# 24 instead of 32 tokens of the expert stage computed from gathered rows, the other 232 by dense products

## The chip, the cores and the metric

The kernel runs on one core of a Trainium2 chip. The metric is the device time of one execution in microseconds, median of the runs. The inputs are fixed by the reference: 256 tokens of width 1024, float32.

## The reference, cut to what matters

One encoder layer: an input projection, two attentions, gates, an output projection, and then the stage that this change is in, a retrieval of single-neuron experts. Each token picks 16 of 16,384 experts for each of 8 heads (128 picks), with a softmax weight for each pick.

```python
s = jnp.einsum('thpd,hpkd->thpk', q, sub_keys)
v_half, i_half = lax.top_k(s, K)
cand = v_half[:, :, 0, :, None] + v_half[:, :, 1, None, :]
top_s, pos = lax.top_k(cand.reshape(TB, PH, K * K), K)
idx = jnp.take_along_axis(cidx.reshape(TB, PH, K * K), pos, axis=-1)
g = jax.nn.softmax(top_s, axis=-1)
u = expert_u[idx]
a = jax.nn.gelu(jnp.einsum('td,thkd->thk', xb, u), approximate=False)
return jnp.einsum('thk,thkd->td', g * a, expert_v[idx])
```

## The kernel before, in words

**Two ways to the same sum.** Most tokens go the dense way: the activation of every one of the 16,384 experts is computed for them, and what was not picked is multiplied by a gate of 0. NU = 256 - APART = 224 tokens do. The last APART = 32 tokens go apart: their picked rows of `peer_u` and `peer_v` are gathered from HBM by indirect DMAs, 128 rows of 4 KB at a time, and multiplied and added on the VectorE (DVE).

**Dense, first stage (U).** 128 tiles of 128 experts. A tile of 512 KB is loaded to one of four `raw` buffers (SP, `load`, L505), the ScalarE (ACT) rounds it to the high part `whi` (L694), the VectorE or the GpSimd (POOL) subtracts that from it to get the low part `wlo` (L974, L1364 and L1366, L634). TensorE (PE) makes, for each of 8 chunks of the width, three products: high by high, high by low, low by high. In tiles 0 to 41, 126 and 127 these are three matmuls of NU columns (L1524, `split_product`). In tiles 42 to 125 ("wide" tiles) the two products with the same stationary operand are one matmul of 2 x NU columns (L1532), followed by one of NU (L1533): a pair. The two halves of a wide tile are added outside: ACT copies one (L850, `take_half`), DVE adds the other (L1358, `add_halves`), ACT applies the GELU (L839), and SP stores the tile to `a_scratch` (L537).

**The gate matrix G.** For tokens 0 to 127 it is scattered to HBM by 128 indirect DMAs of POOL (L667, L669). For tokens 128 to NU - 1 it is made on PE during the wide tiles: one-hot vectors (L1341, L1346 on DVE, L858 on ACT), two matmuls of 256 columns per two tokens (L1787), a copy by ACT (L893) and an add by DVE (L1353, `add_low`). That is G_STEPS = (128 - APART) / 4 = 24 steps of four tokens, three for every eight tiles, from tile 41 to tile 103. In a tile with neither the one-hots of a step nor an `add_low`, DVE splits its subtraction into two halves with `add_halves` between them (`low_halves`, L1360).

**Dense, second stage (V).** 128 tiles of `peer_v`, through the same four buffers. For each, DVE multiplies activations by gates (L1402, `weights`), ACT rounds (L901), DVE subtracts (L1407, `low`) and makes the low part of the `peer_v` tile (L1411, `v_low`). PE makes for each of 8 chunks the pair of 2 x NU and NU columns (L1836, L1837, `v_products`). In the last three tiles, chunk 7 is three matmuls of NU columns instead (L1839). The load of tile i + 4 into a buffer waits until the low part of tile i is made (`load_v`, L582), and the loads of its activations and its G tile wait for `weights` (`load_a`, L587).

**Apart.** The 32 x 128 picks are laid out on 128 partitions as SHARES = 4 groups of 32 tokens with PICKS = 32 columns. So 32 gathers of `peer_u` rows (L644) with 32 dot products (L1377), and 32 gathers of `peer_v` rows (L650) with 32 scaled adds (L1391 and L1394). Six of the `peer_u` gathers are issued during U. The other 26 and the 32 of `peer_v`, 58 in all, come in V, in the order that the string `V_OPS` gives ("d" a dot, "r" a row), one for every 1.9 tiles. The GELU of the dots is applied in three parts (ENDS, GELU_GROUPS). After tile 120, eight products with a column selector of APART columns (L1870) bring the sum into the accumulators. SP loads the picks (L550, 4 DMAs) and the tokens' own vectors (L557, 4 DMAs) during U.

**Order of the work.** Every engine's program is written out by hand, and the engines meet at semaphores. PE waits in V for `lo_ready` and `glo_ready` of the tile at its start (`v_wait`, L1842). SP issues in program order; in the middle and towards the end of V it also loads `h1` (L613 to L616) for the last residual sum.

```python
for half in range(1 if k is None else 2):
    part = range(C) if k is None else range(half * C // 2, (half + 1) * C // 2)
    if wide_now:
        last = halves_product(dst, [(whi[s][:, c, :], wlo[s][:, c, :], xpair[:, :, c, 0:NU]) for c in part], 0 in part, C - 1 in part)
...
pe.matmul(wide[c], whi[s][:, c, :], gpair[s], start=opening, stop=False)
return pe.matmul(acc[c][:, 0:NU], wlo[s][:, c, :], ghi[s], start=False, stop=closing)
```

Of the kernel before, what the change touches and what calls it, by code (L numbers as in the profile page):

```python
# [34 lines left out]
P = 128  # L35
# [9 lines left out]
PH, NK, TOPK = 8, 128, 16  # L45
# [15 lines left out]
T_U = T_QUERY + HP  # L61
# [26 lines left out]

GTOK = 4
GSUB = 2  # L90
APART = 32
G_STEPS = (P - APART) // GTOK
G_FIRST = 41
G_LAST = G_FIRST + (G_STEPS - 1) // 3 * 8 + (G_STEPS - 1) % 3 * 3
# [11 lines left out]


NU = T - APART
SHARES = 4
PARTS = SHARES * APART  # L110
PICKS = 32
DOTS_U = 6
DOT_TILES_U = (76, 84, 92, 100, 110, 117)
GATHERS_U = {3: (0, 1), 4: (2, 3), 5: (4,), 6: (5,)}
ENDS = (0, 6, 18, 32)
WIDE_FIRST, WIDE_END = 42, 126
PICKS_AT, XROWS_AT = 45, 53
OFFSETS_AT = 52
# [1 line left out]
V_SLOT = 512  # L120
NG = NU - P
G_BLOCK = P + NK // RAW * NG
V_OPS = "ddrddrddrddrddrddr" + "dddd" + "dr" * 10 + "r" * 16
OP_FIRST, GATHER_LEAD = 10, 9
GELU_GROUPS = (2, 12, 22)
A_AHEAD_AT = 96


def op_tile(n):

    return OP_FIRST + n * 19 // 10


DOT_AT = {op_tile(n): DOTS_U + V_OPS[:n].count("d") for n in range(len(V_OPS)) if V_OPS[n] == "d"}
ROW_AT = {op_tile(n): V_OPS[:n].count("r") for n in range(len(V_OPS)) if V_OPS[n] == "r"}
SHARES_AT = tuple(min(t for t in ROW_AT if ROW_AT[t] == m) for m in ENDS[:-1])
H_GROUP = 15
# [9 lines left out]
def wide_tile(i):  # L147

    return WIDE_FIRST <= i < WIDE_END


def g_step_at(i):

    at = i - G_FIRST
    if at < 0 or at % 8 not in (0, 3, 6):
        return None
    k = at // 8 * 3 + at % 8 // 3
    return k if k < G_STEPS else None
# [50 lines left out]
def build(nc, stream, urows, vrows, const, keys, bias, lamv, gfin, h1_dram, x_dram, a_dram, g_dram, out):  # L209
    with ExitStack() as top:  # L210
# [3 lines left out]
        def sem(name):  # L214
            return top.enter_context(nc.semaphore(name))

        def sbs(stack, name, shape, dt=F32):
            return stack.enter_context(nc.sbuf_tensor(name, shape, dt))
# [60 lines left out]
                route = sbs(router, "route", [P, TB, 3, PH, TOPK])  # L279
                gsum = sbs(router, "gsum", [P, 2, TB, PH])  # L280
        G = sbs(top, "G", [P, RAW, G_BLOCK])
        held = sbs(top, "held", [P, 128, NK])
        sbs(top, "v_pad", [P, 32])
        vpair = sbs(top, "vpair", [P, RING, V_SLOT], F32R)
        small = sbs(top, "small", [P, T - P - 122, NK])
# [3 lines left out]
        def piece(at, n):  # L289
            return held[:, at:at + n, :].rearrange("p a b -> p (a b)")  # L290
# [3 lines left out]
        def G_at(s, turn, n):  # L294

            if isinstance(turn, int):
                return G[:, s, (turn - 1) * NG:(turn - 1) * NG + n]
            return G[:, s, bass.ds((turn - 1) * NG, n)]
# [4 lines left out]
        xall = piece(76, 8)  # L303
# [3 lines left out]
        ghi = [vpair[:, s, V_SLOT // 2:V_SLOT // 2 + NU] for s in range(RING)]  # L307
        uoff = small[0:P, 2, 0:PICKS].bitcast(U32)
        dots = small[0:P, 2, PICKS:2 * PICKS]
        shares = small[0:P, 2, 2 * PICKS:3 * PICKS]  # L310
        picks = small[0:P, 5, 0:3 * PICKS].rearrange("p (a k) -> p a k", a=3)
        chosen = small[0:P, 3, 0:APART]
        ident2 = small[:, 4, :]
# [21 lines left out]
        result = hT[:].rearrange("p (b x) t -> p b (x t)", b=TB)  # L335
        xtok = qpad[0:APART, 4:8, :].rearrange("p a t -> p (a t)")
        hots = [hot1[:, u] for u in range(HOTS - 1)] + [hot_more[:]]
# [115 lines left out]
        x_landed_apart = sem("x_landed_apart")  # L453
# [35 lines left out]
        def _(sp):  # L489
# [15 lines left out]
            def load(t, s, row):  # L505

                sp.wait_ge(lo_ready, t - RAW + 1)
                sp.dma_start(raw[s][:], row).then_inc(raw_landed[s], 16)
# [25 lines left out]
            def store(i, s2):  # L534

                sp.wait_ge(evac_act, i + (act_takings(T_U) + 1))
                sp.dma_start(a_dram[i] if isinstance(i, int) else a_dram[bass.ds(i, 1)], ast[s2][:]).then_inc(a_stored[s2], 16)  # L537

            def stored(i):

                sp.wait_ge(a_stored[i % AST], 16 * (i // AST + 1))


            def load_picks(g):

                if g == 0:
                    sp.wait_ge(routed, 1)
                n = min(PICKS, PH * TOPK - g * PICKS)
                mine = route[P - APART:P, 1].rearrange("p a h k -> p a (h k)")[:, :, g * PICKS:g * PICKS + n]
                sp.dma_start(picks[g * APART:(g + 1) * APART, :, 0:n], mine).then_inc(picks_landed, 16)  # L550

            def load_xrows(g):

                if g == 0:
                    sp.wait_ge(xtok_stored, 16)
                    sp.wait_ge(gbanks_free, 2)
                sp.dma_start(xall[g * APART:(g + 1) * APART], x_dram).then_inc(x_landed_apart, 16)  # L557

            for t in range(T_U, T_V):
                load(t, t % RAW, stream[t])  # L560
                if t >= T_U + STORE_LAG:
                    store(t - T_U - STORE_LAG, (t - T_U - STORE_LAG) % AST)
                if t == T_U + 1:
                    sp.wait_ge(xtok_ready, 1)
                    sp.dma_start(x_dram, xtok).then_inc(xtok_stored, 16)
                if 0 <= t - T_U - A_AHEAD_AT < 4:
                    q = t - T_U - A_AHEAD_AT
                    stored(q)
                    sp.dma_start(aring[q], a_dram[q]).then_inc(a_landed[q], 16)
                if 0 <= t - T_U - PICKS_AT < SHARES:  # L570
                    load_picks(t - T_U - PICKS_AT)
                if 0 <= t - T_U - XROWS_AT < SHARES:
                    load_xrows(t - T_U - XROWS_AT)
            for s in range(RAW):
                load(T_V + s, s, vrows[s:s + 1])
                i = NE_TILES + s - STORE_LAG
# [14 lines left out]
            for s in range(RAW):  # L591
                load_v(RAW + s, s)
                i = NE_TILES + RAW + s - STORE_LAG
# [33 lines left out]
        def _(pool):  # L627
# [44 lines left out]
            for q in range(4):  # L672
                pool.dma_start(G_at(q, 1, P), g_tiles[q]).then_inc(g_first[q], 16)
            for n in range(len(V_OPS)):
                at = op_tile(n)
# [12 lines left out]
        def _(act):  # L688
# [227 lines left out]
            def gelu_dots(part):  # L916

                act.wait_ge(dots_done, ENDS[part + 1])
                at = slice(ENDS[part], ENDS[part + 1])
                act.activation(dots[:, at], dots[:, at], ACT.Gelu).then_inc(dots_gelu, 1)  # L920

            first = 1
            for part, end in enumerate(GELU_GROUPS):
                groups(first, end)
# [35 lines left out]
        def _(dve):  # L960
# [285 lines left out]
            split = SHORT_X * TOPK  # L1246
# [121 lines left out]
            def offsets_apart():  # L1368

                dve.wait_ge(picks_landed, 16 * SHARES)  # L1370
                dve.scalar_tensor_tensor(uoff, picks[:, 0, :], float(NK), picks[:, 1, :], ALU.mult, ALU.add).then_inc(uoff_ready, 1)

            def dot(j):

                dve.wait_ge(x_landed_apart, 16 * SHARES)
                dve.wait_ge(urow_landed[j % U_BUFS], 16 * (j // U_BUFS + 1))
                dve.scalar_tensor_tensor(urow[j % U_BUFS], urow[j % U_BUFS], 1.0, xall, ALU.mult, ALU.mult, accum_out=dots[:, j:j + 1]).then_inc(dots_done, 1)  # L1377

            def gates_apart(part):

                dve.wait_ge(dots_gelu, part + 1)
                at = slice(ENDS[part], ENDS[part + 1])
                dve.tensor_tensor(shares[:, at], picks[:, 2, at], dots[:, at], ALU.mult).then_inc(shares_ready, 1)

            def add_row(m):

                row = urow[U_BUFS + m % V_BUFS]
                dve.wait_ge(shares_ready, sum(m >= e for e in ENDS[:-1]))
                dve.wait_ge(urow_landed[U_BUFS + m % V_BUFS], 16 * (m // V_BUFS + 1))
# [37 lines left out]
            more_low(T_U + G_FIRST + LO_LEAD - at_lo[0])  # L1427
            for i in range(G_FIRST, NE_TILES):
                before, ahead = g_step_at(i - 1), g_step_at(i + 2)
                split = wide_tile(i - 1) and ahead is None and before is None  # L1430
                if wide_tile(i - 1) and not split:
                    add_halves(i - 1)
                if ahead is not None:
                    one_hots(2 * ahead)
                if before is not None:
                    add_low(before)
                if i == NE_TILES - 1:
                    low(0, 0)
                    low(1, 1)
                if split:  # L1440
                    low_halves(T_U + i + LO_LEAD, i - 1)
                else:
                    low_w(T_U + i + LO_LEAD)
                if ahead is not None:
                    one_hots(2 * ahead + 1)
                j = dot_at(i)
                if i == OFFSETS_AT:
                    offsets_apart()
                if j is not None:
                    dot(j)  # L1450
                if i == G_LAST + 1:
                    dve.wait_ge(gbanks_free, 2 + G_STEPS)
                    dve.wait_ge(g_done, 2 * G_STEPS)
                if i == NE_TILES - 2:
                    weights(0, 0, 1)
                    weights(1, 1, 1)
# [536 lines left out]
```

## Time and profile before

| what | value |
|---|---|
| median of 3 runs | 928.15 us (925.18 to 928.76) |
| the profiled execution | 928.84 us |
| its span, first to last instruction | 927.0 us |
| PE busy | 914.0 us |
| PE weight loads busy | 877.7 us |
| DVE busy | 806.1 us |
| ACT busy | 572.5 us |
| POOL busy | 402.7 us |
| moved by DMA | 261.33 MB |

The profiled execution takes 1.8 us outside its span. Matmuls are pipelined and a recorded matmul is longer than the time until the next one starts, so that a busy PE is not yet a PE at its peak: what a matmul costs in a stream is the distance between starts. The weight loads (PEld) are recorded apart and overlap the matmuls.

### The profile page before, as it was taken

What the parts mean: (1) busy time and instruction counts of PE and PEld (TensorE: products, weight loads), DVE (VectorE), ACT (ScalarE), POOL (GpSimd) and SP (SyncE); (2) the same over time, 40 slices, a digit from 0 to 9 for tenths busy, and PEclk for the clock granted to TensorE, in tenths of its full rate; (3) what the DMA queues carried; (4) which work ended last, traced back from release to release, by engine and by line L of the source; (5) the groups of instructions that cost most, each with busy time, mean ns of one, the idle gap of its engine ahead of it and who ended that gap; (6) DMA issues with size and microseconds to landing.
All of it is one profiled execution on the core that took longest, in us unless ns stands there. A gap on an engine that the chain in (4) does not pass through costs nothing.

```text
span 927.0 us, 20169 instructions
## 1 busy us (share of the span) xinstructions
PE 914.0 (99%) x6644; PEld 877.7 (95%) x6644; DVE 806.1 (87%) x1654; ACT 572.5 (62%) x1059; POOL 402.7 (43%) x234
## 2 busy tenths in 40 slices
PE   9999999999999999999999999999999999999997
PEld 8999889999999999999999999999999899999997
DVE  7988877887799997888999876789999899999886
ACT  6555774666645556888788766555555455555555
POOL 0000000047697786888878867222224223243400
PEclk9999999999999999999999999999999999999999
DMA  8877658566477888999999999999999999999991
GB/s 301 264 236 214 206 176 263 188 225 213 158 250 231 242 242 203 265 285 279 237 256 250 264 261 257 310 402 398 394 381 360 400 394 387 397 338 402 394 306 47
DMA packets 137592, 261.33 MB, mean 282 GB/s; under 512 B 31184, under 2 KB 80208, under 8 KB 137264
## 3 DMA queue, kind: packets, MB, share of 16 engines
q1 hardware_dynamic: 110544, 225.72, 72.6%
q0 software_dynamic: 26544, 33.89, 13.8%
q10 hardware_dynamic: 432, 0.80, 0.3%
q8 instruction: 40, 0.66, 0.3%
q14 instruction: 32, 0.26, 0.1%
HBM read 234.94 MB, written 25.36 MB: 281 GB/s over the span
## 4 chain that ended last, share of the span: by engine, by line
PE 74%; DVE 9%; DMA 7%; issue 4%; ACT 4%; SPq 1%; another core or an unknown queue 0%; DVEq 0%; ACTq 0%
PE pOO L1524 29%; PE pMM L1532 5%; PE pOO L1532 5%; PE pTT L1836 4%; DMA raw<-in_vrows 4%; PE pOO L1836 4%; PE pMM L1836 4%; PE pSS L1836 4%; PE pMM L1533 3%; PE pOO L1533 2%; ACT whis L694 2%; PE pMM L1837 2%; PE pOO L1837 2%; PE pTT L1837 2%; PE pSS L1837 2%
## 5 line engine op out<-in xcount | busy, mean ns | idle before, releaser
L694 ACT ACTIVATE whis<-raw 128x1024 fp32r<-128x1024 f32 x326 | 343.5, 1056 | 148.0 <-PE pSS L1837 77.1
L669 POOL DMA_INDIRECT g_scratch<-small x117 | 211.9, 1811 | 50.3 <-issue 33.9
L1524 PE MATMUL pOO<-xpair,whis 128*128 128x224 f32 (+1 forms) x1184 | 206.6, 279 | 0.3 <-ACT ast L844 0.3
L1524 PEld LDWEIGHTS pOO<-xpair,whis 128*128 128x128 f32 x1184 | 180.7, 191 | 1.9 <-issue 1.8
L1411 DVE TENSOR_TENSOR wlos<-raw,whis 128x1024 fp32r<-128x1024 f32 x125 | 152.9, 1223 | 26.8 <-ACT whis L694 23.7
L634 POOL TENSOR_TENSOR wlos<-raw,whis 128x1024 fp32r<-128x1024 f32 x30 | 72.1, 2410 | 215.4 <-ACT whis L694 215.3
L1524 PE MATMUL pOO<-xpair,wlos 128*128 128x224 f32 (+1 forms) x592 | 164.0, 277 | 0.0
L974 DVE TENSOR_TENSOR wlos<-raw,whis 128x1024 fp32r<-128x1024 f32 x118 | 143.2, 1219 | 5.8 <-ACT whis L694 4.7
L1524 PEld LDWEIGHTS pOO<-xpair,wlos 128*128 128x128 f32 x592 | 112.7, 190 | 0.0
L1532 PE MATMUL pOO<-xpair,whis 128*128 128x448 f32 x336 | 107.4, 373 | 0.5 <-DVE wlos L974 0.4
L1532 PE MATMUL pMM<-xpair,whis 128*128 128x448 f32 x336 | 107.8, 372 | 0.0
L650 POOL DMA_INDIRECT held<-in_vrows,small x32 | 56.4, 1763 | 96.1 <-PE pSS L1837 55.6
L1836 PE MATMUL pTT<-vpair,whis 128*128 128x448 f32 x256 | 88.9, 377 | 4.0 <-DVE vpair L1407 3.8
L644 POOL DMA_INDIRECT held<-in_urows,small x32 | 45.0, 1406 | 106.8 <-PE pSS L1837 86.4
L1533 PE MATMUL pMM<-xpair,wlos 128*128 128x224 f32 x336 | 89.2, 265 | 0.0
L1533 PE MATMUL pOO<-xpair,wlos 128*128 128x224 f32 x336 | 89.2, 265 | 0.0
L1836 PE MATMUL pMM<-vpair,whis 128*128 128x448 f32 x256 | 87.7, 372 | 0.0
L1836 PE MATMUL pOO<-vpair,whis 128*128 128x448 f32 x256 | 87.7, 372 | 0.0
L1836 PE MATMUL pSS<-vpair,whis 128*128 128x448 f32 x253 | 86.8, 372 | 0.0
L1532 PEld LDWEIGHTS pOO<-xpair,whis 128*128 128x128 f32 x336 | 63.0, 187 | 5.9 <-DVE wlos L974 1.3
L1837 PE MATMUL pTT<-vpair,wlos 128*128 128x224 f32 x256 | 67.9, 265 | 0.0
L1837 PE MATMUL pMM<-vpair,wlos 128*128 128x224 f32 x256 | 67.9, 265 | 0.0
(303 smaller groups left out, 2192.9 us busy)
## 6 DMA issues: line engine op xcount, KB each, us to landing
raw<-in_stream SPq DMA_DIRECT2D x199, 512.0 KB
raw<-in_vrows SPq DMA_DIRECT2D x128, 512.0 KB
a_scratch<-ast SPq DMA_DIRECT2D x128, 112.0 KB
held<-a_scratch SPq DMA_DIRECT2D x128, 112.0 KB
g_scratch<-ghot SPq DMA_DIRECT2D x32, 256.0 KB, 4.6
G<-g_scratch SPq DMA_DIRECT2D x124, 64.0 KB
biasm<-in_bias SPq DMA_DIRECT2D x8, 256.0 KB, 5.8
g_scratch<-small POOLq DMA_INDIRECT x128
```

The costliest lines, as they stand in the source:

```text
L634: pool.tensor_tensor(wlo[s], raw[s][:], whi[s].bitcast(F32), ALU.subtract).then_inc(lo_ready, 1)
L644: pool.indirect_dma_start(urow[j % U_BUFS], None, urows, bass.IndirectOffsetOnAxis(uoff[:, j:j + 1], 0)).then_inc(urow_landed[j % U_BUFS], 16)
L650: pool.indirect_dma_start(urow[U_BUFS + m % V_BUFS], None, picked, bass.IndirectOffsetOnAxis(uoff[:, m:m + 1], 0)).then_inc(urow_landed[U_ ...
L669: pool.indirect_dma_start(g_dram, bass.IndirectOffsetOnAxis(goff[:, n:n + 1], 0), gval[:, h, k:k + 1], None, compute_op=ALU.add).then_inc( ...
L694: act.activation(whi[s], raw[s][:], ACT.Copy).then_inc(hi_ready, 1)
L974: dve.tensor_tensor(wlo[t % RING], raw[t % RING][:], whi[t % RING].bitcast(F32), ALU.subtract).then_inc(lo_ready, 1)
L1411: dve.tensor_tensor(wlo[s], raw[s][:], whi[s].bitcast(F32), ALU.subtract).then_inc(lo_ready, 1)
L1524: last = pe.matmul(dst, st, mv, start=(opening and c == 0 and q == 0), stop=(closing and c == len(terms) - 1 and q == 2))
L1532: pe.matmul(both, sh, mv, start=opening and c == 0, stop=False)
L1533: last = pe.matmul(bank[:, 0:NU], sl, mv[:, 0, :], start=False, stop=closing and c == len(terms) - 1)
L1836: pe.matmul(wide[c], whi[s][:, c, :], gpair[s], start=opening, stop=False)
L1837: return pe.matmul(acc[c][:, 0:NU], wlo[s][:, c, :], ghi[s], start=False, stop=closing)
```

## The change

APART goes from 32 to 24, so that NU becomes 232 (pairs of 464 and 232 columns), and with it:

- The picks are laid out as 5 groups of 24 tokens with 26 columns. The gathers of each kind go from 32 to 26; 20 and 26 of them, 46 in all, come in V, one for every 2.4 tiles. The last partitions of a gather (120 to 127) belong to no pick.
- SP loads the picks with 5 DMAs and the tokens' vectors with 6.
- G is made on PE for 104 tokens instead of 96: 26 steps, the last at tile 108.
- The split subtraction is used only after the last step (tiles 110 to 126); before it, a wide tile's add always comes ahead of DVE's subtraction.
- `held` is cut by as many bytes as G grows, so that the operands behind them keep their places.

```diff
-APART = 32
+APART = 24
...
-SHARES = 4
+SHARES = 5
...
-PICKS = 32
+PICKS = 26
...
-ENDS = (0, 6, 18, 32)
+ENDS = (0, 6, 16, 26)
...
-V_OPS = "ddrddrddrddrddrddr" + "dddd" + "dr" * 10 + "r" * 16
+V_OPS = "ddrddrddrddrddrr" + "dddrdrdrdrdrdrdrdrrr" + "r" * 10
...
-GELU_GROUPS = (2, 12, 22)
+GELU_GROUPS = (2, 12, 23)
...
-    return OP_FIRST + n * 19 // 10
+    return OP_FIRST + n * 12 // 5
...
-        held = sbs(top, "held", [P, 128, NK])
+        held = sbs(top, "held", [P, 120, NK])
...
-                sp.dma_start(xall[g * APART:(g + 1) * APART], x_dram).then_inc(x_landed_apart, 16)
+                n = min(APART, P - g * APART)
+                sp.dma_start(xall[g * APART:g * APART + n], x_dram[0:n]).then_inc(x_landed_apart, 16)
...
-                if 0 <= t - T_U - XROWS_AT < SHARES:
+                if 0 <= t - T_U - XROWS_AT <= SHARES:
...
-                dve.wait_ge(x_landed_apart, 16 * SHARES)
+                dve.wait_ge(x_landed_apart, 16 * (SHARES + 1))
...
-                split = wide_tile(i - 1) and ahead is None and before is None
-                if wide_tile(i - 1) and not split:
+                if wide_tile(i - 1) and i <= G_LAST + 1:
                     add_halves(i - 1)
...
-                if split:
+                if i > G_LAST + 1 and wide_tile(i - 1):
                     low_halves(T_U + i + LO_LEAD, i - 1)
```

## Rows read from the trace of the kernel before

**Rows 1.** The page: busy time of each engine, and the chain that ended last.

```profile
PE 914.0 (99%) x6644; PEld 877.7 (95%) x6644; DVE 806.1 (87%) x1654; ACT 572.5 (62%) x1059; POOL 402.7 (43%) x234
...
PE 74%; DVE 9%; DMA 7%; issue 4%; ACT 4%; SPq 1%; another core or an unknown queue 0%; DVEq 0%; ACTq 0%
```

**Rows 2.** Windows: wide tiles of U, its last two tiles, V.

```profile
core 0: us, PE busy (x) PEld busy (x) DVE busy (x) ACT busy (x) POOL busy (x), PEclk, DMA share, GB/s
...
361.20:583.95 222.75, 222.26 (x1437) 211.61 (x1436) 187.67 (x390) 171.08 (x365) 179.24 (x105) 1.00 0.96 258
583.95:589.43 5.48, 5.48 (x50) 5.46 (x50) 3.77 (x10) 3.72 (x8) 0.00 (x0) 1.00 0.94 293
589.43:917.80 328.37, 324.38 (x2062) 307.08 (x2061) 299.04 (x478) 179.59 (x263) 94.60 (x59) 1.00 0.98 363
```

**Rows 3.** Timeline of PE in V: two starts that are 24 pairs apart.

```profile
639.68 0.37 PE L1836 MATMUL pMM<-vpair,whis 128*128 128x448 f32 x1
639.89 0.27 PE L1837 MATMUL pMM<-vpair,wlos 128*128 128x224 f32 x1
...
647.20 0.37 PE L1836 MATMUL pMM<-vpair,whis 128*128 128x448 f32 x1
```

**Rows 4.** Timeline of PE in U's narrow tiles: two starts 63 matmuls apart.

```profile
254.90 0.27 PE L1524 MATMUL pOO<-xpair,wlos 128*128 128x224 f32 x1
...
261.93 0.28 PE L1524 MATMUL pOO<-xpair,wlos 128*128 128x224 f32 x1
```

**Rows 5.** Timeline of PE: 32 columns; and 256 columns, two starts 11 apart.

```profile
896.87 0.61 PE L1870 MATMUL pMM<-small,held 128*128 128x32 f32 x4
897.31 0.61 PE L1870 MATMUL pOO<-small,held 128*128 128x32 f32 x4
...
181.74 0.28 PE L1524 MATMUL pOO<-mhi,whis 128*128 128x256 f32 x1
...
182.99 0.28 PE L1524 MATMUL pOO<-mhi,wlos 128*128 128x256 f32 x1
```

**Rows 6.** The chain in order of time: start, us, what; two of the query tiles.

```profile
229.34 0.87 PE pTT L1776 x8
230.22 2.83 PE pOO L1524 x24
```

**Rows 7.** Groups of instructions by line and shape: the ones that change in number or size.

```profile
L1787 PE MATMUL pSS<-ghot,hot 128*128 128x256 f32 x48 | 9.8, 284 | 0.0
L1411 DVE TENSOR_TENSOR wlos<-raw,whis 128x1024 fp32r<-128x1024 f32 x125 | 152.9, 1223 | 26.8 <-ACT whis L694 23.7 <-issue 2.5
L1402 DVE TENSOR_TENSOR held<-held,G 128x224 f32<-128x224 f32 x128 | 49.3, 386 | 0.3 <-DMA G<-g_scratch 0.3
L1394 DVE SCALAR_TENSOR_TENSOR held<-held,small 128x1024 f32<-128x1024 f32 x31 | 39.7, 1280 | 0.1
L1377 DVE SCALAR_TENSOR_TENSOR held<-held 128x1024 f32<-128x1024 f32 x32 | 39.1, 1221 | 0.0
L1364 DVE TENSOR_TENSOR wlos<-raw,whis 128x512 fp32r<-128x512 f32 x54 | 37.3, 691 | 27.4 <-ACT whis L694 26.6 <-issue 0.8
L1346 DVE TENSOR_SCALAR ghot<-iota,routeT,ghiT 128x128 fp32r<-128x128 f32 x72 | 22.4, 373 | 0.0
L1341 DVE TENSOR_TENSOR hot<-routeT,iota 128x256 fp32r<-128x256 f32 x36 | 15.0, 416 | 0.0
```

**Rows 8.** Waits: what PE and its weight loads waited for in V.

```profile
PE pTT L1836 <- DVE vpair L1407: 3.8, 6, 1.3
...
PEld pTT L1836 <- DVE vpair L1407: 5.3, 7, 1.6
```

**Rows 9.** The chain in order of time, in V, around its longest stall.

```profile
711.10 8.80 DMA G<-g_scratch
...
728.87 0.42 SPq L614
...
729.74 7.56 DMA raw<-in_vrows
```

## The prediction

> **What bounds the kernel now.** I read the page's busy times and its chain first [rows 1]. PE holds 99% of the span and 74% of the chain that ended last; DVE comes next with 87% and 9%. A busy PE proves little, since a recorded matmul outlasts the start of the next, so I took the windows of the two stages that the change touches [rows 2] and, in timelines, the distance between starts [rows 3 to 6].
>
> In V a pair of 448 and 224 columns takes (647.20 - 639.68) / 24 = 0.3133 us [rows 3]. 128 tiles of 8 pairs at that pace are 320.8 us; the 16 products of L1870 add 4 x 0.44 = 1.8 us [rows 5]. The stage lasts 328.37 us [rows 2], so PE lost 5.8 us to waits. In the wide tiles of U, 84 x 8 pairs are 210.5 us, and 23 steps of G with 4 matmuls each, at 2.83 / 24 = 0.118 us [rows 6], are 10.9 us; of the window's 222.75 us that leaves 1.4 us [rows 2]. So PE's own pace sets 98% of both stages, and **7.2 us is all that any relief of DVE, POOL or DMA can give back**. The waits are on DVE's part of a tile [rows 8], and the longest has slow DMA landings around it (8.80 and 7.56 us for loads whose tile is needed four tiles, 10 us, later), just where SP loads `h1` [rows 9].
>
> **What a column costs.** The granted clock is 1.00 everywhere in these windows [rows 2], the 2.4 GHz level. A column per cycle is then 0.4167 ns, my estimate for a column that PE has to wait for. But not every column is one:
> - Narrow tiles: 224 columns take (261.93 - 254.90) / 63 = 0.1116 us [rows 4]. 128 columns take 0.87 / 8 = 0.109, and even 32 take 0.111 us [rows 5, 6]. So there is a floor near 0.111 us per matmul that has nothing to do with columns. 256 columns take 1.25 / 11 = 0.1136 [rows 5] to 0.118 us [rows 6], that is 7 to 11 ns over 256 x 0.4167. For 232 columns this gives 96.7 + 7 to 11 = 104 to 108 ns, under the floor. I take 0 for the 8 more columns here, at most 3.3 ns.
> - Pairs: 672 columns at 0.4167 are 280 ns of the 313.3, so the pair is mostly columns. Lower bound: the matmul of 464 pays its 16 columns and the one of 232 stays at the floor, +6.7 ns. Upper bound: proportional, 24 x 313.3 / 672 = +11.2 ns. I take the plain 24 x 0.4167 = +10.0 ns: after a 448 the next start comes 0.21 us later and after a 224 0.10 us [rows 3], the latter less than the floor, so both seem to pay columns.
>
> The Trainium skill bears on the first point: TensorE: Matmul & The Clock Gate, section LDWEIGHTS, has a weight load take its columns at 1.2 GHz, 107 ns for 128; by an estimate from that page the floor is the weight load, and 232 columns (97 ns) stay behind it, as in my sum. The same page's section Back-to-back issue gap has the gap of an isolated matmul as N / 2.4 + 2.5 ns, which would charge the 8 columns everywhere; here 32 columns at 0.111 us go against using that formula below 256 columns.
>
> **The sum, part by part.**
> 1. Pairs: 84 x 8 = 672 in U, 125 x 8 + 3 x 7 = 1,021 in V, 1,693 together. 1,693 x 10.0 ns = **+16.9 us** (11.3 to 19.0).
> 2. Narrow matmuls: 44 x 24 in U and 9 at the end, 1,065: **0** (to +3.5 us at 3.3 ns).
> 3. Two more steps of G: 8 matmuls x 0.118 to 0.122 us, **+1.0 us**. On DVE a step costs two one-hots of 0.416, four times 0.373 and, for an add of 512 elements, 0.69 us as L1364 has [rows 7], 3.0 us; two are 6 us. Against that, the split goes from 54 tiles [rows 7] to 17 (110 to 126): 2 x 0.69 instead of 1.22 us, so 37 x 0.16 = 5.9 us less. DVE has 187.67 of 222.75 us there [rows 2] and stays where it is. Order: `add_halves` now stands ahead of the subtraction, where DVE sat idle for ACT anyway (27.4 us [rows 7]). Behind it on DVE are the one-hots and `wlo` of tile i + 2; after PE ends tile i - 1, ACT's copy, the add and 1.22 us make about 2 us, while PE needs that `wlo` 5 us after. 0 on the path.
> 4. V, DVE: 6 dots and 6 scaled adds fewer, 6 x 1.221 + 6 x 1.280 = -15.0 us. `weights` and `low` grow by 8 elements at (1223 - 386) / 800 = 1.05 ns [rows 7], 256 x 8.4 ns = +2.1 us. DVE falls from 299 of 328 to 286 of some 337 us. POOL issues 12 gathers fewer.
> 5. V, DMA: 12 gathers of 512 KB fewer, -6.3 MB; 128 loads of activations of 116 instead of 112 KB, +0.5 MB. The window moved 328.37 us x 363 GB/s = 119 MB [rows 2], so 5% less, over a longer stage.
> 6. From 4 and 5, and as a slower PE gives each load 0.3 us more over four tiles, part of the 7.2 us of waits goes. The waits beside the loads of `h1` have a cause that stays, and so does the start of V. I take **-4.0 us** (0 to -7.2).
> 7. SP: 1 + 2 more issues at 0.2 to 0.4 us each [rows 9], between loads of U at the tiles 49, 57 and 58. They delay one load each by that; U's loads have the ring of four tiles as cover. 0; without cover, at most 1 us. L1870's products go from 32 to 24 columns, at the floor: 0. Stores of 116 KB, two `hT` adds with 8 more columns: 0.1 us or less.
>
> Sum: 16.9 + 0 + 1.0 - 4.0 = **+13.9 us**. The profiled execution took 928.84 us, 0.7 above the median of 928.15; against its own time the sum is 942.7, on the median **942.0 us**.
>
> **Rivals.**
> - **A. Only the wide half pays** (+6.7 ns per pair, the matmul of 232 behind its weight load). 11.3 + 1.0 - 4.0 = +8.3: 936.5 us. For it: 0.10 us after a 224 is near the floor. Against: it is already under it.
> - **B. Every column is paid.** The narrow tiles pay 3.3 ns a matmul too, 3.5 us. 16.9 + 3.5 = 20.4; 20.4 + 1.0 - 4.0 = +17.4: 945.5 us. For it: the two kinds differ by little (0.111 and 0.118). Against: the 32 columns. (The Trainium skill, TensorE: Matmul & The Clock Gate, section Back-to-back issue gap, would have it this way if its formula for an isolated matmul held in a stream.)
> - **C. The relief doesn't come.** The gathers are fewer, but the waits belong to `h1` and to the latency of a tile's load, so the waits stay at 7.2 us: 16.9 + 1.0 = +17.9, 946.1 us. For it: [rows 9]. Against: DVE at 91% and fewer bytes.
> - **D. Faster.** In a pair each run of 224 columns costs 0.10 us or more where its columns need 0.093, and if a run of 232 fits into that same time, as 224 and 256 columns nearly do in single matmuls, the pair pays nothing; the waits go with the gathers: +1.0 - 7.2 = -6.2, 922.0 us. It decides from about 3.7 ns per pair downward, (7.2 - 1.0) / 1,693. Against: between 224 and 256 single columns a floor explains the small step, and the pair isn't at a floor.
>
> **How the numbers follow.** The forecast 0.58, A 0.13, B 0.10, C 0.12, D 0.07. The lowest cost with all waits gone is 11.3 + 1.0 - 7.2 = +5.1 (933 us), the highest with none gone 19.0 + 3.5 + 1.0 = +23.5 (952 us). 933 to 950 leaves out D and the far end. A measurement of this kernel can tell about 0.5%, 4.6 us, from no change: faster than that 0.06, within it 0.06, slower 0.88.
>
> **What would show it.** Right: pairs at 0.323 us in V's timeline, narrow matmuls still 0.112, V some 338 us long by the window of its first and last product, U's wide window some 7 us longer plus the steps of G, DVE under 290 us in V, PE's waits on `vpair` under 5 us. A: pairs at 0.320. B: narrow at 0.115. C: waits as before at the same places. D, and my forecast wrong: pairs at 0.317 or less. Wrong too: new waits of PE on `wlos` in the tiles 42 to 110, which would put the order of DVE in part 3 at fault.

## The result, and the profile after

The changed kernel takes 940.33 us (median of 5 runs, 939.98 to 943.58) against 928.15 (925.18 to 934.65): a ratio of 1.0116, 95% interval 1.0073 to 1.0158 (the ratios here and below are the recorded ones with their intervals; the quotient of the two medians is 1.0131). By the medians it is 12.2 us slower; forecast were 13.9, with 942.0 us. The profiled execution has a span of 938.2 us against 927.0.

The page of the changed kernel, busy times and chain:

```profile
PE 929.3 (99%) x6652; PEld 880.0 (94%) x6652; DVE 799.5 (85%) x1613; ACT 576.5 (61%) x1069; POOL 364.8 (39%) x222
...
PE 93%; DVE 3%; issue 1%; ACT 1%; DMA 1%; DVEq 0%; ACTq 0%
```

Set against [rows 1]: DVE has 7 us less to do and POOL 38 us less, and PE now makes up 93% of the chain that ended last, instead of 74%. DVE, DMA and ACT had 20% of the chain together and have 5% now. PE has become nearly the only limit, and a longer one.

The windows that answer to [rows 2]: wide tiles of U, its last two tiles, and V (same columns).

```profile
361.81:591.25 229.44, 229.44 (x1445) 213.35 (x1444) 191.38 (x367) 175.45 (x375) 171.89 (x104) 1.00 0.94 253
591.25:596.79 5.54, 5.54 (x50) 5.48 (x50) 3.76 (x10) 3.77 (x8) 0.00 (x0) 1.00 0.86 243
596.79:929.14 332.35, 332.35 (x2062) 308.32 (x2061) 288.43 (x460) 179.10 (x263) 63.60 (x47) 1.00 0.96 341
```

The wide tiles take 6.7 us longer, V 4.0 us. In V, PE's busy time now equals the window; in [rows 2] it fell 4 us short.

The timelines of PE that answer to [rows 3] (V, two starts 24 pairs apart) and, after the dots, to [rows 4] (narrow tiles, two starts 63 matmuls apart):

```profile
699.69 0.38 PE L1836 MATMUL pSS<-vpair,whis 128*128 128x464 f32 x1
...
707.45 0.38 PE L1836 MATMUL pSS<-vpair,whis 128*128 128x464 f32 x1
...
253.87 0.27 PE L1524 MATMUL pOO<-xpair,wlos 128*128 128x232 f32 x1
...
260.90 0.27 PE L1524 MATMUL pOO<-xpair,wlos 128*128 128x232 f32 x1
```

A pair takes (707.45 - 699.69) / 24 = 0.3233 us, 10.0 ns more than before. A narrow matmul takes 7.03 / 63 = 0.1116 us, the same as before to the last digit.

**Where the 11.2 us of span came from.** From the starts of PE's matmuls in the two traces, stage by stage:

| part | us |
|---|---|
| 1,693 pairs at +10.1 ns on the mean | +17.1 |
| 8 more matmuls for G | +1.0 |
| waits in the wide tiles, 1.3 to 0 | -1.3 |
| waits in V, 6.5 to 0.3 | -6.2 |
| narrow tiles (a stall at 302 to 307 us, below) | +2.0 |
| everything ahead of U, and the end | -1.5 |
| sum | +11.1 |

"Waits" is here and below the sum of what the distance between the starts of two pairs has above the pace of that kernel's pairs. PE waits of the changed kernel, all that V and the wide tiles have left, and the ones in the narrow tiles:

```profile
PEld pOO L1524 <- issue: 3.1, 9, 1.1
...
PE pOO L1524 <- issue: 1.2, 3, 0.9
...
PEld pTT L1836 <- issue: 0.2, 1, 0.2
```

The lines with `vpair` of [rows 8] have no successor. The 2.0 us of the narrow tiles are time in which PE waited for nothing that the profile shows; three later kernels with the same 232 columns there have 0 to 0.4 us at that place, so it belongs to this execution and not to the change.

### The profile page after: what moved, and what is told of

Its sections match the earlier page's. It is cut to its first block, busy times and chain, and to the rows that moved or that the text cites. A ratio compares the mean times of both kernels' runs of the same rounds, so it can differ in the third digit from the quotient of the medians.

```text
span 938.2 us, 20125 instructions
## 1 busy us (share of the span) xinstructions
PE 929.3 (99%) x6652; PEld 880.0 (94%) x6652; DVE 799.5 (85%) x1613; ACT 576.5 (61%) x1069; POOL 364.8 (39%) x222
## 4 chain that ended last, share of the span: by engine, by line
PE 93%; DVE 3%; issue 1%; ACT 1%; DMA 1%; DVEq 0%; ACTq 0%
PE pOO L1524 29%; PE pMM L1532 8%; PE pOO L1532 8%; PE pTT L1836 6%; PE pOO L1836 6%; PE pMM L1836 6%; PE pSS L1836 6%; PE pOO L1533 4%; PE pMM L1533 4%; PE pOO L1837 3%; PE pTT L1837 3%; PE pMM L1837 3%; PE pSS L1837 3%; DVE wlos L975 1%; PE pSS L1598 1%
## 5 line engine op out<-in xcount | busy, mean ns | idle before, releaser
L1524 PE MATMUL pOO<-xpair,whis 128*128 128x232 f32 (+1 forms) x1184 | 207.2, 279 | 1.1 <-issue 1.1
L975 DVE TENSOR_TENSOR wlos<-raw,whis 128x1024 fp32r<-128x1024 f32 x155 | 188.3, 1218 | 14.3 <-ACT whis L695 11.2
L1524 PE MATMUL pOO<-xpair,wlos 128*128 128x232 f32 (+1 forms) x592 | 164.1, 277 | 0.2 <-issue 0.2
L1532 PE MATMUL pMM<-xpair,whis 128*128 128x464 f32 x336 | 111.4, 379 | 0.0
L1532 PE MATMUL pOO<-xpair,whis 128*128 128x464 f32 x336 | 110.3, 379 | 0.0
L1533 PE MATMUL pOO<-xpair,wlos 128*128 128x232 f32 x336 | 90.9, 270 | 0.0
L1533 PE MATMUL pMM<-xpair,wlos 128*128 128x232 f32 x336 | 90.8, 270 | 0.0
L1836 PE MATMUL pTT<-vpair,whis 128*128 128x464 f32 x256 | 89.8, 379 | 0.0
L1836 PE MATMUL pMM<-vpair,whis 128*128 128x464 f32 x256 | 89.5, 379 | 0.0
L1836 PE MATMUL pOO<-vpair,whis 128*128 128x464 f32 x256 | 89.5, 378 | 0.0
L1836 PE MATMUL pSS<-vpair,whis 128*128 128x464 f32 x253 | 88.6, 379 | 0.0
```

Of the source, the lines that this page charges most:

```text
L975: dve.tensor_tensor(wlo[t % RING], raw[t % RING][:], whi[t % RING].bitcast(F32), ALU.subtract).then_inc(lo_ready, 1)
L1524: last = pe.matmul(dst, st, mv, start=(opening and c == 0 and q == 0), stop=(closing and c == len(terms) - 1 and q == 2))
L1532: pe.matmul(both, sh, mv, start=opening and c == 0, stop=False)
L1533: last = pe.matmul(bank[:, 0:NU], sl, mv[:, 0, :], start=False, stop=closing and c == len(terms) - 1)
```

## The experiments

### The two halves of the relief: gathers and pace

The kernel before was timed again beside each set of experiments, on the same chip: 927.74 us beside those of this section and the next, 929.12 us beside the order of DVE and the first two with `h1` in pieces, 928.45 us beside the last two. The ratios are against these.

The forecast let 4.0 of 7.2 us of waits go; nearly all went. Two edits separate the gathers from the slower pace of PE. First, 232 columns with the old number of gathers:

```diff
-PICKS = 26
+PICKS = 32
+PICK_W = 26
...
-V_OPS = "ddrddrddrddrddrr" + "dddrdrdrdrdrdrdrdrrr" + "r" * 10
+V_OPS = "ddrddrddrddrddrddr" + "dddd" + "dr" * 10 + "r" * 16
...
-    return OP_FIRST + n * 12 // 5
+    return OP_FIRST + n * 19 // 10
```

> The changed kernel (232 columns) with the gathers, dots and scaled adds of before again: 32 of each kind, 58 in V, one per 1.9 tiles. The six extra columns gather the rows of the first six again and have a gate of 0. Theory G (the waits of before went because 12 gathers and their DVE work went): PE's waits in V come back, 5 to 7 us, so about 946 us against 940.3 of the change. Rival P (they went because PE takes 0.32 instead of 0.31 us per pair, which gives each load of the ring of four more time): V stays without waits, 940 to 941 us.

Measured: 943.12 us (941.99 to 944.01), ratio 1.0173 (1.0133 to 1.0214). Second, 224 columns with the new, thinner schedule of gathers:

```diff
-V_OPS = "ddrddrddrddrddrddr" + "dddd" + "dr" * 10 + "r" * 16
+V_OPS = "ddrddrddrddrddrr" + "dddrdrdrdrdrdrdrdrrr" + "r" * 10
...
-    return OP_FIRST + n * 19 // 10
+    return OP_FIRST + n * 12 // 5
...
-            pe.wait_ge(rows_added, PICKS)
+            pe.wait_ge(rows_added, TAKEN)
```

> The kernel before (224 columns) with the schedule of 26 gathers of each kind of the change, 46 in V; the picks of the columns 26 to 31 are left out of the sum. Theory G: the 5.8 us of waits of V go, 921 to 923 us against 928. Rival P: the waits stay as they were, 927 to 928 us. If both have a part, it lies between.

Measured: 923.99 us, ratio 0.9955 (0.9934 to 0.9976); nine of the ten runs took 922.83 to 926.17 us and one 2,902 us, for which nothing on record gives a reason and which is not in the ratio. The windows of V, from its first product on, of the kernel with 232 columns and the old gathers (to 0.8 us before its last product):

```profile
595.20:931.00 335.80, 334.11 (x2061) 308.23 (x2060) 301.17 (x478) 180.85 (x263) 90.78 (x59) 1.00 0.98 356
```

and of the one with 224 columns and the new ones:

```profile
588.60:915.90 327.30, 324.01 (x2068) 307.79 (x2067) 286.63 (x461) 178.97 (x264) 65.44 (x48) 1.00 0.96 345
```

PE's waits in V, one profile each:

| | 58 operations | 46 operations |
|---|---|---|
| 448 and 224 columns | 6.5 us | 4.7 us |
| 464 and 232 columns | 3.8 us | 0.3 us |

Both theories had a part and neither was right alone. At either width fewer gathers take 1.8 to 3.5 us off, and at either number of gathers the slower pairs take 2.7 to 4.4 us off. The 4.7 us are likely on the high side, since the profiled run of that kernel (926.17 us) is its longest of the nine. The ring of four tiles accounts for both: the load of tile i + 4 begins when tile i's low part is made and has four tiles to land, be rounded and be subtracted. Slower pairs lengthen those four tiles by 0.3 us, 32 pairs at 10 ns. Fewer gathers shorten the landing. The median from issue to landing of a `peer_v` tile, the last number, with 58 operations in V and 232 columns, and with 46 operations and all but the same pace (a kernel of the next section):

```profile
raw<-in_vrows SPq DMA_DIRECT2D x128, 512.0 KB, 6.6
```

```profile
raw<-in_vrows SPq DMA_DIRECT2D x128, 512.0 KB, 5.8
```

With 224 columns in V it is 6.4 us with 58 operations (the ladder of the next section, whose V is that of the kernel before) and 5.7 us with 46.

What ACT waited for such a tile to land, in the kernel before, in the one with 232 columns and the old gathers, in the one with 224 columns and the new ones, and in the changed one:

```profile
ACT whis L694 <- DMA raw<-in_vrows: 47.0, 38, 2.7
```

```profile
ACT whis L696 <- DMA raw<-in_vrows: 37.0, 30, 3.0
```

```profile
ACT whis L695 <- DMA raw<-in_vrows: 28.3, 22, 4.4
```

```profile
ACT whis L695 <- DMA raw<-in_vrows: 18.3, 14, 2.2
```

Each half of the relief lowers ACT's waits too: from 47.0 us, slower pairs alone to 37.0, fewer gathers alone to 28.3, both to 18.3. But the sum of them doesn't give PE's waits. Of the two kernels in the middle, the one with the smaller sum (28.3) has more waits of PE (4.7 against 3.8 us): its longest single wait of ACT is 4.4 us, until 600.2 us, and right behind it, at 600.9 us, PE lost 2.1 us at once. What PE loses is what single loads have over their room, and not their sum.

### What a column of a pair costs

Rival A had it that only the first matmul of a pair pays. The changed kernel, with the second cut back:

```diff
-                    last = pe.matmul(bank[:, 0:NU], sl, mv[:, 0, :], start=False, stop=closing and c == len(terms) - 1)
+                    last = pe.matmul(bank[:, 0:NU - 8], sl, mv[:, 0, 0:NU - 8], start=False, stop=closing and c == len(terms) - 1)
...
-                return pe.matmul(acc[c][:, 0:NU], wlo[s][:, c, :], ghi[s], start=False, stop=closing)
+                return pe.matmul(acc[c][:, 0:NU - 8], wlo[s][:, c, :], ghi[s][:, 0:NU - 8], start=False, stop=closing)
```

> The changed kernel with the second matmul of every pair (low part of the weights) cut back to 224 columns, the first at 464; so the tokens 224 to 231 lack that product. If the second matmul pays its columns: pairs at 320 ns instead of 323.4, 1,693 x 3.3 ns = 5.6 us less, about 935 us. If it sits at the floor of a single matmul (rival A of the prediction): pairs at 323, 940 us.

Measured: 936.77 us (936.39 to 938.66), ratio 1.0109 (1.0067 to 1.015), between the two readings. Its timeline in V, two starts 24 pairs apart:

```profile
699.74 0.39 PE L1836 MATMUL pSS<-vpair,whis 128*128 128x464 f32 x1
...
707.47 0.38 PE L1836 MATMUL pSS<-vpair,whis 128*128 128x464 f32 x1
```

A pair takes 0.3221 us (mean 321.6 ns in U, 322.2 in V), 1.2 to 1.8 ns less than the 323.4 ns with 232, where a plain column rate wants 3.3. So 8 columns of the second matmul cost about half of that rate or less, and the 16 of the first cost 8.6 to 8.8 ns, more than their 6.7. The time fell by more (3.6 us, between medians on two chips and between the two profiles) than 1,693 x 1.5 ns = 2.5 us. In the profiles the other 1.1 us lie ahead of the wide tiles, where the changed kernel has its stall at 302 to 307 us; between the medians they aren't explained.

To get the other widths too, the widths of the kernel before went round from tile to tile in U, with unread columns added:

```diff
+LADDER = (224, 232, 240, 248, 256)
+PAIRS = ((224, 224), (232, 232), (240, 240), (256, 256), (240, 224), (256, 224), (256, 240))
...
-                act.activation(ast[i % AST][:], wide_u[(i - WIDE_FIRST) % 4][:, NU:2 * NU], ACT.Copy).then_inc(half_taken, 1)
+                act.activation(ast[i % AST][:], wide_u[(i - WIDE_FIRST) % 4][:, T:T + NU], ACT.Copy).then_inc(half_taken, 1)
```

> The kernel before, but with widths that go round from tile to tile in U, the added columns unread. Narrow tiles: 224, 232, 240, 248, 256 columns by tile number modulo 5. Wide tiles: pairs of 2 x 224 and 224, 2 x 232 and 232, 2 x 240 and 240, 2 x 256 and 256, 2 x 240 and 224, 2 x 256 and 224, 2 x 256 and 240 modulo 7. Theory: single matmuls stay at 111.5 ns up to 240 columns, 248 at 112 to 114, 256 at 114 to 118. Pairs by 0.4167 ns a column from 313.3: 323, 333, 353, and 327, 340, 347 ns for the mixed ones. If the second matmul of a pair were at a floor, the mixed pairs (240, 224) and (256, 224) would be within 2 ns of (240, 240) and (256, 240). Time some 930 to 945 us, of no use by itself.

Its timeline, the first matmul of each of eight tiles in a row (eight pairs each; the second matmuls have 224, 240, 224, 232, 240, 256, 224 and 224 columns):

```profile
554.58 0.40 PE L1547 MATMUL pOO<-xpair,whis 128*128 128x512 f32 x1
...
557.33 0.40 PE L1547 MATMUL pOO<-xpair,whis 128*128 128x512 f32 x1
...
560.08 0.37 PE L1547 MATMUL pMM<-xpair,whis 128*128 128x448 f32 x1
...
562.58 0.38 PE L1547 MATMUL pMM<-xpair,whis 128*128 128x464 f32 x1
...
565.18 0.38 PE L1547 MATMUL pOO<-xpair,whis 128*128 128x480 f32 x1
...
567.82 0.40 PE L1547 MATMUL pOO<-xpair,whis 128*128 128x512 f32 x1
...
570.62 0.38 PE L1547 MATMUL pMM<-xpair,whis 128*128 128x480 f32 x1
...
573.25 0.40 PE L1547 MATMUL pMM<-xpair,whis 128*128 128x512 f32 x1
```

An eighth of a distance is a pair: 2.50 / 8 = 0.3125 us for 448 and 224, 2.75 / 8 = 0.344 for 512 with 224 and for 512 with 240 alike, 0.350 for 512 and 256. The means over all tiles of a kind (some 80 pairs each, 184 to 229 narrow matmuls each), from the one run that was made, of 939.67 us:

| first, second | ns a pair | | narrow | ns |
|---|---|---|---|---|
| 448, 224 | 313.1 | | 224 | 111.3 |
| 464, 232 | 324.3 | | 232 | 111.9 |
| 480, 224 | 327.4 | | 240 | 111.9 |
| 480, 240 | 330.1 | | 248 | 115.7 |
| 512, 224 | 342.3 | | 256 | 118.4 |
| 512, 240 | 343.2 | | | |
| 512, 256 | 349.7 | | | |

Up to 240 columns the narrow matmuls came as expected; 248 columns took 115.7 ns where 112 to 114 were expected, and 256 took 118.4, just over the expected 118. The end of the floor lies between 240 and 248 columns. With the first fixed, the second matmul from 224 to 240 columns adds only 1 to 3 ns, and from 240 to 256 another 6.5: in a pair, too, the second matmul sits near the floor up to 240. The first pays all of it: from 448 to 480 and to 512 columns 14.3 and 14.9 ns, 0.45 to 0.47 ns a column, above the 0.4167 that I had taken. (The Trainium skill, TensorE: Matmul & The Clock Gate, section LDWEIGHTS, gives a weight load of 128 columns P / 1.2, 107 ns. The floor here is 111.3 to 111.9 ns, near that and not equal to it. No run here changes the weight load, so that it makes the floor is not shown.) The expectation of 327 and 340 ns for two of the mixed pairs was nearly met (327.4 and 342.3), and still the reading "columns count in both" was wrong: the two errors, of the first matmul and of the second, cancel. The third mixed pair tells them apart: 512 and 240 columns took 343.2 ns, 1 ns over 512 and 224, where that reading wanted 347.

### The order of DVE

Part 3 of the prediction put the new place of `add_halves` at 0. Taken alone, on the kernel before:

```diff
-                split = wide_tile(i - 1) and ahead is None and before is None
-                if wide_tile(i - 1) and not split:
+                if wide_tile(i - 1) and i <= G_LAST + 1:
...
-                if split:
+                if i > G_LAST + 1 and wide_tile(i - 1):
```

> The kernel before with the change's order of DVE alone: add_halves ahead of an unsplit subtraction up to the last step of G. Part 3 of the prediction puts this at 0. If the three waits of 0.3 to 0.6 us in the wide tiles before (at the dots) went because of the order, 926.5 us and no waits of PE in the wide window; if they went because of the slower pairs, they stay and the time is 927.7 us.

and taken back, on the changed kernel:

> The changed kernel with DVE's order of before (the split subtraction in every wide tile without one-hots or add_low). If the order had no part, 940.3 us and no waits in the wide window. If the order keeps the wide tiles free of waits, waits of 0.3 to 0.6 us come back at the dots, 941 to 942 us.

Measured: 930.8 us against 929.12, ratio 1.0006 (0.9983 to 1.0029), and 940.61 us (939.06 to 943.05), ratio 1.0107 (1.0079 to 1.0135) where the change has 1.0116. In the wide tiles neither has a wait left, while the kernel before has 1.3 us: either the order or the slower pairs is enough there. For the changed kernel the order is worth nothing that these runs can tell. The first of them showed no gain either, though its interval doesn't exclude 1.3 us. Its profile, of the longest of its twelve runs (934.65 us), shows what can take the gain away. Its timeline of PE, from the last product of U to the first of V, and the windows around it:

```profile
587.74 0.27 PE L1523 MATMUL pOO<-xpair,wlos 128*128 128x224 f32 x1
593.17 0.71 PE L1835 MATMUL pTT<-vpair,whis 128*128 128x448 f32 x1 [5.16 <-DVE vpair L1407]
593.68 0.39 PE L1836 MATMUL pTT<-vpair,wlos 128*128 128x224 f32 x1
593.87 0.60 PE L1835 MATMUL pTT<-vpair,whis 128*128 128x448 f32 x1
```

```profile
587.00:591.00 4.00, 1.01 (x10) 0.83 (x8) 0.00 (x0) 0.00 (x0) 2.28 (x4) 1.00 0.83 248
591.00:594.00 3.00, 0.83 (x3) 0.82 (x4) 2.06 (x5) 1.86 (x5) 0.00 (x0) 0.53 0.25 72
594.00:598.00 4.00, 4.00 (x16) 3.69 (x15) 3.64 (x6) 1.36 (x3) 0.00 (x0) 0.50 0.58 169
598.00:602.00 4.00, 4.00 (x27) 3.81 (x27) 1.95 (x4) 2.55 (x4) 2.06 (x2) 1.00 0.93 260
```

PE stands 5.2 us. When it resumes, and until 598 us, the granted clock is 0.50, the 1.2 GHz level, and a pair takes 0.59 us. Its chain says what V waited for:

```profile
581.07 5.66 DMA g_scratch<-small
...
587.02 4.60 DMA G<-g_scratch
591.72 0.40 DVE held L1402
```

V's first tiles need G, and G needs the last of POOL's 128 scatters. In the profiles of the 224-column kernels POOL issues the first G load between 580 and 587 us, and U ends at 588 to 589 (the ladder, with wider tiles in U, at 603). In those with 232 columns it does so between 575 and 581 us, and U ends at 594 to 597. The kernel before, and the changed kernel:

```profile
575.78 1.55 POOL L669 DMA_INDIRECT g_scratch<-small  x1 [0.30 <-issue]
581.16 2.28 POOL L673 DMA_DIRECT2D G<-g_scratch  x4 [3.83 <-DMA g_scratch<-small]
```

```profile
569.23 1.55 POOL L670 DMA_INDIRECT g_scratch<-small  x1 [0.30 <-issue]
574.75 2.28 POOL L674 DMA_DIRECT2D G<-g_scratch  x4 [3.96 <-DMA g_scratch<-small]
```

In the stalled profile V's first product came 593.17 - 587.02 = 6.15 us after this issue. By the same distance the kernel before could have started V at 587.3 us and did at 589.43, so it had some 2 us of room; the changed kernel could have at 580.9 and did at 596.79, some 16 us of room (8 to 12 in the three other kernels with 232 columns). So the kernel before stands at the edge of a second limit that its own profile doesn't show, because in that execution the scatters were just in time.

The mean granted clock of each run gives a hint how often the limit was hit, since 6.8 us at 0.50 take 0.004 off it. With the order alone on the kernel before, the six longest runs of twelve (930.96 to 934.65 us) have a clock of 0.995 or 0.996, and the other six 0.997 to 1.000 with a median of 928.72 us. Of the kernel before, only 2 of 29 runs on the same chip have 0.996, and its four longest (932.51 to 933.84 us) have 0.997 or 0.999. The runs of the changed kernel lie closer together (939.98 to 943.58) than those of the kernel before (924.6 to 934.7 over all chips). So late starts of V with a fall of the clock can account for the long runs of the new order, but not for the longest ones of the kernel before, whose cause stays open.

### Can the waits be had without the columns?

The longest waits of [rows 9] lie around the loads of `h1`. In eight pieces, on the kernel before:

```diff
-            sp.dma_start(hT[:, 0:HALF, :], h1_dram[:, 0:HALF, :]).then_inc(final_landed, 16)
-            groups(H_GROUP, TAKE_GROUP)
-            sp.dma_start(hT[:, HALF:C, :], h1_dram[:, HALF:C, :]).then_inc(final_landed, 16)
-            groups(TAKE_GROUP, NE_TILES // RAW)
+            for c in range(C):
+                sp.dma_start(hT[:, c, :], h1_dram[:, c, :]).then_inc(final_landed, 16)
+                if c < C - 1:
+                    groups(H_GROUP + 2 * c, H_GROUP + 2 * c + 2)
+            groups(H_GROUP + 2 * C - 2, NE_TILES // RAW)
```

> The kernel before with h1 loaded in eight pieces of 128 KB, two groups of four tiles apart, instead of two of 512 KB. If the waits in the middle and near the end of V (the 1.0 us and 0.3 us after the first load in the profile before, 0.5 and 0.7 us around the second) come from these loads, they go: 925.5 to 926.5 us against 927.7. If they come from the gathers' density alone, the time stays at 927 to 928 us, with waits at other places.

Measured: 926.12 us against 929.12, ratio 0.9964 (0.9944 to 0.9983). It is the only kernel here that computes everything and is faster than the kernel before by more than the noise, and it beats the changed one by some 1.5%. Its waits in V are 3.2 us instead of 6.5, and those near the end of V are gone; the kernel with the order alone, where `h1` is still loaded in two pieces, has 2.5 us of them at 877 to 888 us. Not in the 3.2 are 1.9 us of idle PE at the start of V and 1.7 us more from the lower clock behind it, in the profiled run (928.70 us, above the median). Adding the order of DVE:

> Both on the kernel before: h1 in pieces and the change's order of DVE. A candidate that beats both kernels: if each gives what its theory has, 1.5 and 1.0 us, 925 us; the sum of all waits of PE in U and V, 7.2 us, is the bound, 921 us.

Measured: 928.12 us, ratio 0.9984 (0.9962 to 1.0006): no gain clear of the noise; its profile (929.48 us) has 4.5 us of idle PE at the start of V. Then two gathers were taken out from among the scatters, to bring the scatters' end forward:

```diff
-DOTS_U = 6
+DOTS_U = 4
...
-GATHERS_U = {3: (0, 1), 4: (2, 3), 5: (4,), 6: (5,)}
+GATHERS_U = {3: (0, 1), 4: (2, 3)}
...
-V_OPS = "ddrddrddrddrddrddr" + "dddd" + "dr" * 10 + "r" * 16
+V_OPS = "ddr" * 4 + "d" * 12 + "dr" * 8 + "r" * 20
```

> The kernel before with h1 in pieces, the change's order of DVE, and only four of the six peer_u gathers issued between the scatters of G in U; the other two come in V, 60 operations there instead of 58. Theory S (the start of V in the 224-column kernels hangs on the end of POOL's scatters, whose last DMA and the first G tiles came 0 to 5 us late in the profiles of the three kernels with h1 in pieces or the new order): two gathers fewer on POOL, 2 x 1.85 us, bring the first G tiles 3.7 us earlier, V starts without a wait, 923 to 925 us against 928.1 of the kernel with the first two edits alone, and the runs lie closer together. If the wait at V's start was chance, or two more operations in V cost what this gives, 927 to 929 us.

> The same without the change's order of DVE: h1 in pieces and four gathers in U. The waits of some 1 us in the wide tiles stay. Theory S: 924 to 926 us. Otherwise 926 to 928 us, as with h1 in pieces alone (926.1).

Both missed, on the slow side of either theory: 931.87 us, ratio 1.004 (1.0025 to 1.0055), and 929.56, ratio 1.0012 (0.9995 to 1.0028). The scatters ended no earlier. Timeline of POOL of the first of the two:

```profile
568.02 1.92 POOL L670 DMA_INDIRECT g_scratch<-small  x1 [0.30 <-issue]
575.86 1.60 POOL L670 DMA_INDIRECT g_scratch<-small  x1 [5.92 <-issue]
```

In every profile here POOL's scatters start 0.30 us after the one before has ended, but for seven pauses of 2 to 8 us in which POOL waits for earlier scatters to land. In these two kernels there is an eighth, of 5.9 us (4.1 us in the other kernel, behind the same scatter), in which POOL waits for nothing that the profile shows. It is longer than the 3.7 us that were to be won. Its cause is open. Code loading isn't supported: both profiles have 34 instead of 32 packets on the second queue of kind "instruction", but so have the two other kernels with `h1` in pieces, which have no such pause. And with two more operations in V its waits are 8.0 and 4.7 us, where the same kernels without the move have 2.2 and 3.2. In the first of the two, nine of twelve runs have a granted clock of 0.994 to 0.996, a sign of a late start of V in most of them. What the start of V would give when it is never late stays open.

## Why the prediction was right

The forecast had the right mechanism, PE's own pace with part of its waits going. Two things in the sum were off, and that the total came so near is in part luck: inside step 1 two errors cancel, and step 6 was too small by half.

- **PE bounds both stages, and 7.2 us is all that relief can give**: held in the main. 7.5 us of waits went by the starts, and PE's own pace set the rest. The 7.2 were a little low: the window that I had taken ends 0.8 us before V's last product, and by the starts there were 6.5 + 1.3 = 7.8 us of waits.
- **Step 1, pairs, +10.0 ns and +16.9 us**: measured +10.1 ns and +17.1 us. The size was right, its make-up not. "Both seem to pay columns" fails: 8 columns of the second matmul cost 1.2 to 1.8 ns and not 3.3, 16 of the first 8.6 to 8.8 and not 6.7. Of rival A the mechanism was nearer than mine, but its price for the first matmul was too low. My reason was the 0.10 us after a 224, less than the floor. That distance alone tells nothing: with a first matmul of 512 columns, as the second goes from 224 to 240, the mean distance after the second grows from 103.4 to 111.0 ns and the one after the first falls from 238.9 to 232.2. Only their sum is a price.
- **Step 2, narrow tiles, 0**: held to 0.1 ns. Rival B falls.
- **Step 3, G and the order, +1.0 and 0**: held for the time. The order removes the 1.3 us of waits in U at 224 columns, which I hadn't foreseen, and nothing at 232. DVE's part was misread: its busy time in the wide tiles rose from 187.67 to 191.38 us where the sum had nearly nothing. Records of DVE overlap the next one by 0.08 us. From start to start a half subtraction takes 0.60 us and a whole one 1.14, so that a split costs 0.06 us and not 0.16, and 37 of them 2.2 us and not 5.9. As PE has no wait in the changed kernel's wide tiles, it cost nothing.
- **Step 4, DVE to 286 us in V**: 288.4.
- **Step 5, bytes in V, 5% less**: 332.35 us x 341 GB/s = 113 MB against 119, held.
- **Step 6, waits, -4.0**: the term that was off, -7.5. I kept part of the waits because they lie beside the loads of `h1`, a cause that stays. The cause did stay, but a wait is an excess over the room that a load has; gathers and pace each took 2 to 4 us of waits off, and together nearly all. Rival C falls.
- **Step 7, 0**: no wait is left in the wide tiles, where the three more issues of SP lie.
- **Rival D** (a pair pays nothing) falls by the same 10 ns. It had the right end for the waits.
- **One sign was set wrong**: V was to be some 338 us long and measured 332.35. The 338 are 328.37 plus 1,021 pairs at 10.0 ns, without the relief of step 6.
- The missed 1.7 us are step 6 (-3.5) and step 1 (+0.2), with +2.0 and -1.5 us of this one profile's other stages, and the 1 us by which the median moved more than the span.

## What to carry to other kernels

Ask of each column whether the engine pays for it: with 128x128 weights, single matmuls of 224 to 240 columns all took 111.3 to 111.9 ns here, while the wide ones of a pair paid 0.45 ns a column or more, so a wider token block is free in one loop and 17 us dear in another. When PE holds 98% of a stage, add up what its waits are worth before giving it work to relieve others: here 7.5 us against 18.

A wait is an excess over slack, not a property of the transfer beside it: two small reliefs together removed what neither did alone (one profile of each). And a chain that is just in time in the one profile at hand (here POOL's scatters) can turn a saving ahead of it into a wait, with a slower clock behind it.

## What the runs showed of the hardware

- The floor of a single matmul holds to 240 columns (111.9 ns), 248 take 115.7 and 256 take 118.4. In the query stage the same 256-column matmuls took 115.7 ns on the mean in the profile before and 113.8 in the one after, with nothing changed there.
- In the five profiles in which PE stood 1.8 to 5.2 us before V, the granted clock went to the 1.2 GHz level for 3.4 to 6.8 us, most of it with PE busy again; behind the shortest of these stops it fell 1 us after PE had resumed. That cost 1.7 to 2.3 us on top of the idle time itself.
- The landing of a 512 KB tile in V took 6.4 to 6.6 us in the median with 58 gathers beside it and 5.7 to 5.8 us with 46.
- A pause of 4 to 6 us of POOL between two indirect DMAs, for nothing that the profile shows, came in the two kernels with four gathers in U and in none of the ten others. Why isn't known.
